# Moving SBUF buffers by 64 and 128 bytes in a three-block fp32 network: what the phase of an operand is worth

## The chip, the cores and the metric

The kernel runs on one core of a Trainium2 chip. The metric is the device time of one execution in microseconds (us). The three runs of the kernel before took 1833.24, 1834.17 and 1839.31 us, median 1834.17 us.

## What is computed

Three network blocks follow one another on the same 256 tokens of width 1024, in float32. Cut to its core, the reference is:

```python
x = first_block(x, c, ctx, ...)   # modulation, w_in and w_out, retention, then the expert part:
    gate, idx = lax.top_k(jnp.swapaxes(aff, 1, 2), cap)          # 16 experts take 32 tokens each
    a = jnp.einsum('becd,edf->becf', xs, w_gate)                 # 1024 -> 2048
    u = jnp.einsum('becd,edf->becf', xs, w_up)
    y = jnp.einsum('becf,efd->becd', jax.nn.silu(a) * u, w_down)
x = second_block(x, ...)          # state-space and recurrent branches, then a 3072-wide FFN
return third_block(x, ...)        # gated linear + sliding-window attention, then block attention
```

Outside the experts the work is dense products `h @ W` with W of 1024 rows, for all 256 tokens. The experts need 16 x 24 MB of weights, once each.

## The kernel before, in words

**A weight unit.** A dense matrix is cut into units of 1024 rows by 128 columns: eight tiles of 128x128, 4 KB per partition. Four units are one block of 2 MB. Blocks come through `ring`, four slots of 16 KB per partition, by DMA from the SP queue, in one fixed order.

**Two halves of a number.** TensorE multiplies in its rounded form of float32 (fp32r). To keep the precision, weights and activations are each split in a rounded high part and the rest. ScalarE writes a unit's high part from `ring` into one of the four buffers of `w_high` (line 2121 is the helper that records all of ScalarE's operations), VectorE then overwrites the unit in `ring` with its low part (lines 2437 and 2448). The activation's high part lies in `HH` (h_high in the trace), its low part in `H` (h_normed); further on both lie in `U` (work), in some norms in `SQ` (squares).

**A narrow unit.** `dense_unit` then makes 24 matmuls of 256 columns: eight with `w_high` as stationary operand on the high activations, eight with `w_high` on the low ones, eight with the low weights in `ring` on the high ones. The activations (1 KB per partition and tile) are the moving operand. `dense_together` does the same for several units tile by tile. There are 5616 such matmuls; all matmuls of these helpers stand at line 1644.

**A wide unit.** `dense_tokens` turns the roles round: 128 tokens of the activation are stationary, and the weights of four units are the moving operand, four runs of 128 columns (512 in all). There are 192 of these, and 48 with two units (256 columns).

**The experts.** Lines 2077, 2057 and again 1644: plain float32, the activations of 32 tokens stationary in `work` and `ring` moving, 512 columns.

**Where the buffers lie.** `sb` and `sb_split` take SBUF from a rising address, one buffer behind the other in the order of the calls; a buffer of 64 bytes per partition that nothing reads (`between_tables`, `behind_weights`) only moves what lies behind it. Inside a buffer every tile step is a multiple of 512 bytes, so that all tiles of a buffer have the buffer's phase modulo 256. The order of instructions on every engine is written out by hand and waits on semaphores; no address takes part in it.

Of the kernel before, what the change touches and what calls it, by code (L numbers as in the profile page):

```python
# [12 lines left out]
U32 = mybir.dt.uint32  # L13
# [4 lines left out]
P = 128  # L18
SEQ = 256
DM = 1024  # L20
KT = DM // P
# [3 lines left out]
EXPERTS = 16  # L25
CAP = 2 * SEQ // EXPERTS
# [66 lines left out]
HIGHS = 4  # L93
# [58 lines left out]
def d1_block(unit):  # L152

    return FIRST.index(("dense", unit // UNITS))
# [7 lines left out]
def block_ends(unit):  # L162
    return unit % UNITS == UNITS - 1
# [26 lines left out]
def program(nc, d, out):  # L190
    ctx = ExitStack()
    with ctx:
        def sb(name, shape, dt=F32):
            return ctx.enter_context(nc.sbuf_tensor(name, shape, dt))

        rounded = {}

        def sb_split(name, shape):

            buffer = sb(name, shape)  # L200
            size = 4 * math.prod(shape[1:])
            rounded[name] = nc.alloc_sbuf_tensor_at(name + "_rounded", shape, F32R, offset=nc.sbuf_base - size)
            return buffer
# [3 lines left out]
        B = [ctx.enter_context(nc.psum_tensor(f"bank{i}", [P, 512], F32)) for i in range(8)]  # L207

        ring = sb_split("ring", [P, RING, BLK])
        params = sb("params", [P, P_COLS])  # L210
        consts = sb("consts", [P, C_COLS])
        sb("between_tables", [P, 16])
        X = sb("x_resid", [P, KT, SEQ])
        H = sb_split("h_normed", [P, KT, SEQ])
        SQ = sb_split("squares", [P, KT, SEQ])
        RS = sb("rstd", [P, 2, SEQ])
        U = sb_split("work", [P, 80 * SEQ])
        ones = sb("ones", [P, P])
        sm = sb("small", [P, 844])
        w_high_plain = sb_split("weights_high", [P, HIGHS, KT * P])  # L220
        w_high = rounded["weights_high"]
        sb("behind_weights", [P, 16])
        idx_u = sb("topk_index", [EXPERTS, CAP], U32)
        HH_plain = sb_split("h_high", [P, KT, SEQ])
        HH = rounded["h_high"]

        def par(name, a=None, b=None):
            at, n = P_AT[name]
            return params[:, at + (0 if a is None else a):at + (n if b is None else b)]
# [5 lines left out]
        def tiles(a, n):  # L235
            return U[:, a * SEQ:(a + n) * SEQ]
# [4 lines left out]
        def small(at, n):  # L241
            return sm[:, at:at + n]
# [17 lines left out]
        def by_tile(ap):  # L260
            return [ap[:, k, :] for k in range(ap.shape[1])]
# [5 lines left out]
        def as_r(ap):  # L267

            return bass.AP(rounded[ap.tensor.name], ap.offset, ap.ap)
# [54 lines left out]
        ROT = tiles(76, 4)  # L324
        KW = SQ[:, :, :].rearrange("p (s t x) n -> p s t (x n)", s=2, t=TT)
        SFB = tiles(76, 4).rearrange("p (s h c) -> p s h c", s=2, h=HEADS1)
# [40 lines left out]
        w_room = w_high_plain[:, :, :].rearrange("p n c -> p (n c)")  # L367
        h_high, squares, h_normed = (a[:, :, :].rearrange("p k t -> p (k t)") for a in (HH_plain, SQ, H))
        AHEAD = ((w_room[:, 0:DEXP], w_room[:, DEXP:2 * DEXP]), (tiles(64, 8), tiles(72, 8)),
# [14 lines left out]
        I_OF = (8, 9, 10, 11, 76, 77, 78, 79)  # L384
        XDT = SQ[:, :, :].rearrange("p (t x) n -> p t (x n)", t=TT)
        DTT = small(112, 32).rearrange("p (t h) -> p t h", t=TT)
# [31 lines left out]
        def d2_block(unit):  # L418
            return D2_BLOCK0 + unit // UNITS
# [33 lines left out]
        def tensor_block2(pe, mm, dense_unit, dense_together, added_token_sums, spread_roots):  # L453
            def unit2(unit, act, name=None):
                tensor_dense2(pe, dense_unit, unit, act, PU2 + unit, base=IN_AT[name][0] if name else None)

            normed = by_tile(HH), by_tile(as_r(H[:, :, :]))

# [68 lines left out]
            for g in range(2):  # L527
                last = mm(B[4 + g][:, 0:SEQ], ones[:], SQ[:, 4 * g, :])
            last.then_inc(s.ya_sum, 1)
            for n in range(5, 8):  # L530
                unit2(L_LRU + n, lru)
            ssm = by_tile(as_r(SQ[:, :, :])), by_tile(as_r(YA))
            for n in range(8):
# [25 lines left out]
        def scalar_block2(act, fn, link, square, squares_of_x, raw_splits, root_table, root, unit_done, weight_high, split_high):  # L559
# [95 lines left out]
            for n in range(4):  # L655
# [6 lines left out]
                if n == 2:  # L662
                    act.wait_ge(s.ya_gated, 1)
                    fn(flat(SQ), tiles(53, 8), ACT.Square).then_inc(s.ya_act, 1)
                if n < 3:
# [62 lines left out]
        def vector_block2(dve, v, link, norm_invert, norm_to, add_normed, split_low, split_scaled_low, weight_low, weights_low):  # L728
# [182 lines left out]
            dve.wait_ge(s.dense_sb, PU2 + L_UP)  # L911
            add_normed(6, MO2, after=lambda k: split_scaled_low(H[:, k, :], X[:, k, :], par("ffn_pre", k, k + 1), HH_plain[:, k, :]))
            weight_low(L_UP - 1 + AHEAD2)
# [43 lines left out]
            dve.wait_ge(s.dense_sb, PU2 + L_DOWN + KT)  # L957
            add_normed(8, DO, after=lambda k: split_scaled_low(H[:, k, :], X[:, k, :], EVEN_GAIN[:, k:k + 1], HH_plain[:, k, :]))
            weight_low(L_EVEN - 1 + AHEAD2)
# [44 lines left out]
        def tensor_block3(pe, mm, dense_unit, dense_together, dense_tokens, added_sums, added_token_sums, spread_roots):  # L1004
            normed = by_tile(HH), by_tile(as_r(H[:, :, :]))

# [163 lines left out]
        def scalar_block3(act, fn, link, squares_of_x, raw_splits, root_table, root, unit_done, weight_high, split_high, splits_apart):  # L1170
# [111 lines left out]
            for n in range(RAW_UNITS):  # L1282
                for k in (2 * n, 2 * n + 1):
                    split_high(HH[:, k, :], H[:, k, :])
                unit_done(d2_block(L_ODD + n), block_ends(L_ODD + n))
# [28 lines left out]
        def vector_block3(dve, v, link, norm_invert, norm_to, final_norm, split_low, split_scaled_low, times_rstd, weight_low, weights_low):  # L1314
# [161 lines left out]
            for k in range(KT):  # L1476
                if k + 1 < KT:
                    times_rstd(10, H, X, RAW_GAIN, k + 1).then_inc(s.act_full, 1)
                split_low(H[:, k, :], HH[:, k, :])
                if k % 2 == 0:  # L1480
# [161 lines left out]
        def _(pe):  # L1642
# [196 lines left out]
            def first_jobs():  # L1839

                ctx_base, x_base = IN_AT["ctx"][0], IN_AT["x"][0]
                ctx_high, ctx_low = by_tile(as_r(CTXR)), by_tile(as_r(HC))
                x_high, x_low = by_tile(HH), by_tile(as_r(H[:, :, :]))
                by_unit = lambda ap: ap.rearrange("p (u k c) -> p u k c", u=UNITS, k=KT)
# [37 lines left out]
            for pu, (unit, act, t) in enumerate(DENSE1):  # L1882
# [3 lines left out]
                blk, sub = d1_block(unit), unit % UNITS  # L1886
                high, low = (HH, H[:, :, :]) if act == "x" else (as_r(CTXR), HC)
                high, low = by_tile(high), by_tile(as_r(low))
# [990 lines left out]
```

## Time and profile before

| what | value |
|---|---|
| median of three runs | 1834.17 us |
| the profiled execution, its own time | 1832.58 us |
| its span in the trace | 1830.8 us |
| TensorE matmuls busy | 80% of the span |
| VectorE, ScalarE, GpSimd busy | 39%, 32%, 2% |
| first stretch, first block's dense work | 0 to about 230 us |
| experts | about 250 to 1130 us |
| second and third block | about 1130 us to the end |

TensorE's row counts a matmul as busy from its start to the end of its pipeline, so that neighbours overlap; the pace of a train of matmuls is read from the starts of two rows and the number of matmuls between them. In the list of rows by time a row merges neighbouring instructions of one kind: its start, its length, and how many.

### The profile page before, as it was taken

The page shows a single profiled execution, that of the slowest core. Times are in us where ns is not written, and L with a number is a line of the kernel's source. Part 1 is how long each engine was busy: PE and PEld are TensorE (multiplying, and loading weights), DVE is VectorE, ACT ScalarE, POOL GpSimd, SP SyncE. Part 2 cuts the span into 40 slices and gives each one's busy share as a digit, 9 for nine tenths or more (in the row PEclk, how much of TensorE's full clock was granted, in tenths as well). Part 3 has the DMA queues.
Part 4 walks back from the last instruction along what each step waited for, and adds up shares of the span by engine and source line. Part 5 has one row for each costly group of instructions (what it writes and reads, how often), then busy time and mean ns, then how long its engine had stood idle before and what let it go on. Part 6 is the DMA issues. An engine that isn't in the chain of part 4 may idle for free.

```text
span 1830.8 us, 25067 instructions
## 1 busy us (share of the span) xinstructions
PE 1462.0 (80%) x10432; PEld 990.6 (54%) x10432; DVE 710.5 (39%) x1256; ACT 589.2 (32%) x1007; POOL 35.6 (2%) x40
## 2 busy tenths in 40 slices
PE   6999996665656666666656667999999999999998
PEld 4787941211112111112111112998998999999997
DVE  4457610000000000000000000897995999478764
ACT  6444510000000000000000001677475776465654
POOL 0000200000000000000000000000000000000101
PEclk9999897888887787877878877999999999999999
DMA  9566799999999999999999999657453755554330
GB/s 399 221 246 235 301 386 424 428 428 429 429 429 428 428 429 428 429 428 428 428 429 429 429 428 427 242 188 207 154 185 132 267 206 190 191 173 173 139 139 24
DMA packets 53266, 573.55 MB, mean 313 GB/s; under 512 B 4928, under 2 KB 15424, under 8 KB 16576
## 3 DMA queue, kind: packets, MB, share of 16 engines
q1 hardware_dynamic: 47440, 563.10, 75.7%
q10 hardware_dynamic: 5744, 9.28, 1.4%
q8 instruction: 61, 1.00, 0.2%
q14 instruction: 21, 0.17, 0.0%
HBM read 568.04 MB, written 4.33 MB: 313 GB/s over the span
## 4 chain that ended last, share of the span: by engine, by line
DMA 43%; PE 37%; DVE 16%; ACT 2%; issue 1%; SPq 0%; DVEq 0%; ACTq 0%
PE bank L1644 36%; DMA ring<-in_w_up 14%; DMA ring<-in_w_down 14%; DMA ring<-in_w_gate 13%; DVE ring_rounded L2437 6%; DVE work L929 2%; DVE work L747 1%; DMA ring<-in_dense 1%; DVE work L919 1%; DVE work_rounded L2360 1%; DMA work<-decay_rows 1%; ACT work L2121 1%; DVE work L738 1%; ACT weights_high_rounded L2121 1%; DMA ring<-in_w_ada 1%
## 5 line engine op out<-in xcount | busy, mean ns | idle before, releaser
L1644 PE MATMUL bank<-ring,work 128*32 128x512 f32 x3008 | 483.9, 778 | 293.5 <-DMA ring<-in_w_up 126.3
L1644 PEld LDWEIGHTS bank<-ring,work 128*32 128x32 f32 x3008 | 94.1, 127 | 646.8 <-DMA ring<-in_w_up 206.6
L2121 ACT ACTIVATE work<-bank 128x512 f32<-128x512 f32 (+3 forms) x152 | 72.8, 492 | 998.6 <-PE bank L1644 667.9
L2437 DVE TENSOR_TENSOR ring_rounded<-ring,weights_high_rounded 128x1024 fp32r<-128x1024 f32 x208 | 252.6, 1219 | 80.9 <-ACT weights_high_rounded L2121 80.9
L2121 ACT ACTIVATE weights_high_rounded<-ring 128x1024 fp32r<-128x1024 f32 x244 | 254.0, 1051 | 42.7 <-PE bank L1644 41.4
L2691 DVE TENSOR_TENSOR work<-work,bank 128x512 f32<-128x512 f32 x16 | 16.5, 1030 | 582.7 <-PE bank L1644 582.7
L1644 PE MATMUL bank<-h_high_rounded,weights_high_rounded 128*128 128x256 f32 x1264 | 185.5, 286 | 1.7 <-ACT h_high_rounded L2121 1.5
L1644 PE MATMUL bank<-h_high_rounded,ring_rounded 128*128 128x256 f32 x1264 | 174.5, 277 | 2.4 <-DVE ring_rounded L2448 2.4
L1644 PE MATMUL bank<-h_normed_rounded,weights_high_rounded 128*128 128x256 f32 x1264 | 173.7, 278 | 0.0
L1644 PEld LDWEIGHTS bank<-h_high_rounded,weights_high_rounded 128*128 128x128 f32 x1264 | 161.3, 188 | 13.2 <-issue 6.9
L1644 PEld LDWEIGHTS bank<-h_high_rounded,ring_rounded 128*128 128x128 f32 x1264 | 158.3, 188 | 2.9 <-DVE ring_rounded L2448 2.8
L1644 PEld LDWEIGHTS bank<-h_normed_rounded,weights_high_rounded 128*128 128x128 f32 x1264 | 157.9, 188 | 0.2
L1644 PE MATMUL bank<-work_rounded,weights_high_rounded 128*128 128x256 f32 x1152 | 152.1, 283 | 5.3 <-ACT work_rounded L2121 5.3
L1644 PEld LDWEIGHTS bank<-work_rounded,weights_high_rounded 128*128 128x128 f32 x1152 | 141.9, 192 | 9.4 <-ACT work_rounded L2121 6.9
L2705 DVE COPY work<-bank 128x512 f32<-128x512 f32 x16 | 11.1, 692 | 284.0 <-PE bank L1644 284.0
L2077 PE MATMUL bank<-work 128*128 128x256 f32 x256 | 70.1, 434 | 13.5 <-DVE work L2705 13.5
L2077 PEld LDWEIGHTS bank<-work 128*128 128x128 f32 x256 | 55.0, 221 | 44.2 <-issue 35.1
L1644 PE MATMUL bank<-work_rounded,ring_rounded 128*128 128x256 f32 x544 | 74.5, 280 | 0.0
L1644 PEld LDWEIGHTS bank<-work_rounded,ring_rounded 128*128 128x128 f32 x544 | 68.3, 191 | 0.0
L1627 POOL TENSOR_TENSOR squares<-squares 128x256 f32<-128x256 f32 x30 | 30.1, 1005 | 1770.8 <-ACT squares L2121 1770.8
L2448 DVE TENSOR_TENSOR ring_rounded<-ring,weights_high_rounded 128x1024 fp32r<-128x1024 f32 x36 | 43.6, 1221 | 44.1 <-ACT weights_high_rounded L2121 43.8
L2121 ACT ACTIVATE work<-work,params 128x256 f32<-128x256 f32 x85 | 48.5, 581 | 27.3 <-DVE work L738 17.8
(269 smaller groups left out, 1206.4 us busy)
## 6 DMA issues: line engine op xcount, KB each, us to landing
ring<-in_w_gate SPq DMA_DIRECT2D x63, 2048.0 KB, 16.2
ring<-in_w_down SPq DMA_DIRECT2D x63, 2048.0 KB, 16.2
ring<-in_w_up SPq DMA_DIRECT2D x61, 2048.0 KB, 16.3
ring<-in_dense SPq DMA_DIRECT2D x60, 2048.0 KB, 8.4
ring<-in_w_ada SPq DMA_DIRECT2D x12, 2048.0 KB, 13.5
work<-in_w_up SPq DMA_DIRECT2D x3, 1024.0 KB, 14.6
bias_diagonals<-work SPq DMA_DIRECT2D x2, 1536.0 KB, 14.9
ring<-in_dense SPq DMA_DIRECT2D x2, 1024.0 KB, 18.7
```

The source lines that it names most:

```text
L738: v.tensor_tensor(dst, B[(PU2 + u) % 4][:, 0:SEQ], RS[:, 1, :], ALU.mult).then_inc(s.dense_sb, 1)
L747: v.scalar_tensor_tensor(out=o[:, shift:SEQ], in0=SCALED2[:, u % 4, 0:SEQ - shift], scalar=w[:, 3 - shift:4 - shift], in1=o[:, shift:SEQ], ...
L919: v.tensor_tensor(SCALED[:, u % 4, :], B[(PU2 + L_UP + u) % 4][:, 0:SEQ], RS[:, 1, :], ALU.mult).then_inc(s.dense_sb, 1)
L929: v.scalar_tensor_tensor(out=o[:, shift:SEQ], in0=SCALED[:, u % 4, 0:SEQ - shift], scalar=ffn_weight(u, 2 - shift), in1=o[:, shift:SEQ], o ...
L1627: nc.gpsimd.tensor_tensor(SQ[:, 0, :], SQ[:, 0, :], SQ[:, k, :], ALU.add).then_inc(s.squares_added, 1)
L1644: return nc.tensor.matmul(o, lhsT, rhs, start=start, stop=stop)
L2077: last = nc.tensor.matmul(B[4 + k // 2][:, (k % 2) * SEQ:(k % 2 + 1) * SEQ], YE[:, k * P:(k + 1) * P], SELT[:], start=False, stop=final an ...
L2121: return nc.scalar.activation(o, i, f, **kw)
L2360: v.tensor_tensor(as_r(full), full, as_r(high) if high.dtype == F32 else high, ALU.subtract).then_inc(s.act_low, 1)
L2437: v.tensor_tensor(as_r(w), w, w_high[:, buffer, :], ALU.subtract).then_inc(s.w_low, 1)
L2448: v.tensor_tensor(as_r(w), w, w_high[:, unit % HIGHS, :], ALU.subtract).then_inc(s.w_low, 1)
L2691: v.tensor_tensor(HID.rearrange("p (i q) -> p q i", i=4), rows_apart(SG), rows_apart(B[1][:]), ALU.mult).then_inc(s.hid_ready, 1)
```

## The change

Buffers are allocated in another order, and the two unused 64-byte buffers are gone. Nothing else is edited: the list of instructions of every engine is the same row for row.

```diff
         ring = sb_split("ring", [P, RING, BLK])
+        w_high_plain = sb_split("weights_high", [P, HIGHS, KT * P])
+        w_high = rounded["weights_high"]
         params = sb("params", [P, P_COLS])
         consts = sb("consts", [P, C_COLS])
-        sb("between_tables", [P, 16])
+        idx_u = sb("topk_index", [EXPERTS, CAP], U32)
         X = sb("x_resid", [P, KT, SEQ])
         H = sb_split("h_normed", [P, KT, SEQ])
+        HH_plain = sb_split("h_high", [P, KT, SEQ])
+        HH = rounded["h_high"]
         SQ = sb_split("squares", [P, KT, SEQ])
         RS = sb("rstd", [P, 2, SEQ])
         U = sb_split("work", [P, 80 * SEQ])
         ones = sb("ones", [P, P])
         sm = sb("small", [P, 844])
-        w_high_plain = sb_split("weights_high", [P, HIGHS, KT * P])
-        w_high = rounded["weights_high"]
-        sb("behind_weights", [P, 16])
-        idx_u = sb("topk_index", [EXPERTS, CAP], U32)
-        HH_plain = sb_split("h_high", [P, KT, SEQ])
-        HH = rounded["h_high"]
```

The start of each buffer in a partition, in bytes, worked out from the sizes:

| buffer | before | modulo 256 | now | modulo 256 |
|---|---|---|---|---|
| ring | 16512 | 128 | 16512 | 128 |
| weights_high | 204544 | 0 | 82048 | 128 |
| params | 82048 | 128 | 98432 | 128 |
| consts | 85856 | 96 | 102240 | 96 |
| x_resid | 92096 | 192 | 108544 | 0 |
| h_normed | 100288 | 192 | 116736 | 0 |
| h_high | 221120 | 192 | 124928 | 0 |
| squares | 108480 | 192 | 133120 | 0 |
| rstd | 116672 | 192 | 141312 | 0 |
| work | 118720 | 192 | 143360 | 0 |
| ones | 200640 | 192 | 225280 | 0 |
| small | 201152 | 192 | 225792 | 0 |

## Rows read from the trace of the kernel before

**Rows 1.** Busy time of each engine in stretches (count in brackets), clock, DMA share, GB/s
```profile
0.00:100.00 100.00, 83.35 (x530) 63.14 (x534) 46.02 (x74) 52.09 (x97) 0.20 (x4) 1.00 0.77 312
100.00:230.00 130.00, 124.41 (x907) 109.56 (x897) 85.73 (x164) 57.85 (x109) 11.12 (x12) 0.95 0.65 257
250.00:1130.00 880.00, 557.28 (x3252) 157.77 (x3248) 32.69 (x61) 32.89 (x53) 0.00 (x0) 0.80 1.01 428
1130.00:1831.00 701.00, 677.67 (x5608) 654.11 (x5600) 543.03 (x951) 445.19 (x747) 24.26 (x24) 0.99 0.50 179
1450.00:1500.00 50.00, 50.00 (x444) 50.00 (x443) 48.95 (x95) 36.21 (x56) 0.00 (x0) 1.00 0.57 204
```

**Rows 2.** Costliest groups: busy us, mean ns | idle before, releaser
```profile
L1644 PE MATMUL bank<-ring,work 128*32 128x512 f32 x3008 | 483.9, 778 | 293.5 <-DMA ring<-in_w_up 126.3
...
L2437 DVE TENSOR_TENSOR ring_rounded<-ring,weights_high_rounded 128x1024 fp32r<-128x1024 f32 x208 | 252.6, 1219 | 80.9 <-ACT weights_high_rounded L2121 80.9
```

**Rows 3.** TensorE by time, a train of narrow units in work
```profile
1560.57 1.98 PE L1644 MATMUL bank<-work_rounded,weights_high_rounded 128*128 128x256 f32 x16
1562.39 1.07 PE L1644 MATMUL bank<-work_rounded,ring_rounded 128*128 128x256 f32 x8
1563.29 1.98 PE L1644 MATMUL bank<-work_rounded,weights_high_rounded 128*128 128x256 f32 x16
```

**Rows 4.** TensorE by time, another train, at 1628 us
```profile
1628.39 1.10 PE L1644 MATMUL bank<-h_normed_rounded,weights_high_rounded 128*128 128x256 f32 x8
1629.34 1.10 PE L1644 MATMUL bank<-h_high_rounded,ring_rounded 128*128 128x256 f32 x8
1630.28 1.10 PE L1644 MATMUL bank<-h_high_rounded,weights_high_rounded 128*128 128x256 f32 x8
1631.22 1.10 PE L1644 MATMUL bank<-h_normed_rounded,weights_high_rounded 128*128 128x256 f32 x8
```

**Rows 5.** Durations by buffer, ns min/median/max: 1628 to 1646 us, then 1426 to 1500 us
```profile
L1644 PE MATMUL bank<-h_normed_rounded,weights_high_rounded x54: 279/281/281, 1628.4 to 1645.9; 128*128 128x256 f32 x54
...
L1644 PE MATMUL bank<-h_normed_rounded,weights_high_rounded x216: 276/276/276, 1426.6 to 1498.1; 128*128 128x256 f32 x108
```

**Rows 6.** First and last longer train of the second kind, by time
```profile
102.28 1.10 PE L1644 MATMUL bank<-h_normed_rounded,weights_high_rounded 128*128 128x256 f32 x8
...
1768.15 1.11 PE L1644 MATMUL bank<-h_normed_rounded,weights_high_rounded 128*128 128x256 f32 x8
```

**Rows 7.** TensorE by time, wide units at 75 us
```profile
75.27 2.00 PE L1644 MATMUL bank<-weights_high_rounded,h_high_rounded 128*128 128x512 f32 x8
77.10 1.99 PE L1644 MATMUL bank<-weights_high_rounded,h_normed_rounded 128*128 128x512 f32 x8
78.93 2.03 PE L1644 MATMUL bank<-ring_rounded,h_high_rounded 128*128 128x512 f32 x8
80.80 2.00 PE L1644 MATMUL bank<-weights_high_rounded,h_high_rounded 128*128 128x512 f32 x8
```

**Rows 8.** Matmuls with two columns, by time, then their durations (ns min/median/max)
```profile
1685.42 1.84 PE L1644 MATMUL bank<-ones,work 128*128 128x2 f32 x16
...
L1644 PE MATMUL bank<-ones,work x16: 165/251/251, 1685.4 to 1687.0; 128*128 128x2 f32 x16
```

**Rows 9.** VectorE by line and shape: busy us, mean ns | idle before
```profile
L2360 DVE TENSOR_TENSOR work_rounded<-work,work_rounded 128x256 fp32r<-128x256 f32 x72 | 29.0, 418 | 3.4 <-ACT work_rounded L2121 3.2
```

**Rows 10.** The chain that ended last, 1130 us to the end, its share by line
```profile
by line: PE bank L1644 48.1%; DVE ring_rounded L2437 14.7%; DVE work L929 5.4%; DVE work L747 3.5%; DMA ring<-in_w_down 2.5%; issue 2.4%; DVE work L919 2.3%; DVE work_rounded L2360 1.9%; DMA work<-decay_rows 1.9%; DVE work L738 1.7%; DVE wo
```

**Rows 11.** DMA issues: count, KB each, median us from issue to landing
```profile
weights_high<-in_w_gate SPq DMA_DIRECT2D x2, 1024.0 KB, 10.2
...
h_high<-in_w_up SPq DMA_DIRECT2D x1, 1024.0 KB, 18.5
```

## The prediction, made before the changed kernel ran

> **What bounds the kernel now.** I read three views in this order. First the stretches [rows 1]: from 250 to 1130 us the DMA engines are full (share 1.01, 428 GB/s) while TensorE's weight loads are busy for only 158 of 880 us; from 1130 us to the end TensorE is busy for 678 of 701 us and the DMA half idle. So the experts are bound by the transfers, and what lies ahead of 230 us and behind 1130 us mostly by TensorE's instruction stream. Then the groups [rows 2]: in the experts the matmuls wait 293 us for the ring, so nothing that happens to their pace can show. Last the chain that ended last [rows 10]: of the 701 us behind the experts 48% are matmuls of line 1644, 15% VectorE's making of low weights, and the rest short steps of a norm or a scan. VectorE is a close second: between 1450 and 1500 us it is busy for 48.95 of 50 us [rows 1]. A faster TensorE would soon run into it there; a slower one would be paid nearly in full.
>
> **The change part by part.** No instruction, wait or transfer is added, removed or moved. What changes are starts modulo 256 bytes: the weights' high parts go from 0 to 128, the ring stays at 128, all activations go from 192 to 0. Five kinds of access could notice.
>
> *Narrow units, 5616 matmuls.* Their pace is read from starts. In [rows 3] 24 matmuls go from 1560.57 to 1563.29 us: 2.72/24 = 113.3 ns. In [rows 4] 24 go from 1628.39 to 1631.22: 2.83/24 = 117.9 ns. Both are uninterrupted trains at full clock, on the same buffers' phases. The duration marks the kinds as well: 276 ns in every matmul of the one, median 281 in the other [rows 5]. So there are two paces, and a train keeps the one with which it began until its next gap. Going through all starts in this manner I count 4089 gaps at the fast pace and 1285 at the slow one, which occurs from 101 to 1781 us [rows 6]; the rest are real waits. Within one train the pace does not change when the stationary operand goes from `w_high` at 0 to the ring at 128: in [rows 4] eight from the ring take 0.94 us (1629.34 to 1630.28) and eight from `w_high` take 0.94 us. Thus for narrow units half the change, 0 to 128 for `w_high`, is seen to be worth nothing against activations at 192. The other half, activations at 0, no narrow matmul of this trace shows.
>
> The bounds of it come from the nearest rows. Below: matmuls with two columns are paced by their weight loads alone, and 16 of them take (1.84 - 0.165)/15 = 111.7 ns each [rows 8]. If no moving read ever disturbed anything the narrow units would run at that: 4089 x 1.6 ns = 6.5 us and 1285 x 6.2 = 8.0 us, together 14.5 us. Above: if every train fell in the slow pace, 4089 x 4.6 = 18.8 us. The mean of wide units (below) per 256 columns, 117 ns at most, is no worse than that, so I take 118 as the upper bound of the pace.
>
> *Wide units, 192 matmuls.* Here a phase does show. With the activations stationary at 192 in all three rows, eight matmuls with `w_high` (0) moving take 1.83 us (75.27 to 77.10, and again to 78.93), 228.8 ns each, and eight with the ring (128) moving take 1.87 us (78.93 to 80.80), 233.8 ns [rows 7]. The change puts both at 128 against 0. I expect between 229 for all (64 x 5 ns = 0.3 us less) and 234 for all (128 x 5 = 0.6 us more): nothing, but it is the proof that the start of an operand modulo 256 can matter to TensorE at all, by some 2%.
>
> At this place a rule can be set against the rows. The Trainium skill, page "SBUF — State Buffer", section "SBUF: two separate sides", says that contention on the engines' side comes only from the port pair of VectorE and GpSimd and that TensorE never waits on anyone; "TensorE: Matmul & The Clock Gate", section "Step-by-step: what each phase is for", says that loading the next weights takes no read bandwidth from the running matmul. By these rules placement is worth exactly zero, which is the result of the first rival below too. The trace agrees only in part: with the same code the pace of wide units differs by 5 ns with the buffer read.
>
> *VectorE and ScalarE.* The low-weights step reads the ring (128) and `w_high` (0) and takes 1219 ns for 1024 elements [rows 2]; the same operation on activations (192 and 192) takes 418 ns for 256 [rows 9]. The difference is 801 ns for 768 elements, 1.04 ns each, in one straight line through two different pairs of phases, so I charge 0. After the change the two operands of the first are both at 128; were that to cost what it may, the equal phases of the second (192 and 192) bound it at nothing again.
>
> *Transfers.* The ring stays at its very address, so the experts' 880 us at 428 GB/s stay. Six of the 1 MB loads of the first expert change the phase of their target [rows 11]; they are queued in the saturated stretch's beginning, and a per cent of about 2.4 us each (1 MB at 428 GB/s) is 0.15 us: 0.
>
> *Experts' matmuls.* Their moving operand, the ring, stays, and their stationary one moves from 192 to 0; covered by 293 us of waiting for the ring [rows 2]. Cost 0.
>
> The sum for unchanged paces is thus 0 to -0.3 us on the profiled execution's 1832.58 us (span 1830.8 and 1.8 around it), and the median of the runs lies 1.6 us above that execution. Since which trains fall in the slow pace depends on how they start, I also expect a few us between executions. I say 1833 us.
>
> **The rivals.** What can be told from no change is about 0.3%, 5.5 us.
>
> *A, paces as now (the forecast), 0.38.* For it: 113.3 and 117.9 do not care about 0 or 128 on the stationary side, and both paces exist at one placement, so the start in time decides. Time 1829 to 1838.
>
> *B, activations at 0 are better, 0.32.* The slow pace vanishes, or the fast one drops toward 111.7. The first alone gives 1285 x 4.6 = 5.9 us; the long slow trains lie in stretches that the chain runs through TensorE, so most of it counts: 1828. Both together give at most 14.5 us, of which VectorE's limit around 1450 to 1550 takes a third: 1823 or so. For it: in wide units a moving operand at 0 is faster than one at 128. Against it: there the weights, now at 128, are what moves, and the fast pace stands only 1.6 ns above the load's own floor, so there is little to win.
>
> *C, they are worse, 0.30.* Weights at 128 and activations at 0 make the slow pace the one in which trains end. It decides from the point where over 30% of the 4089 fast gaps turn slow (30% x 18.8 = 5.6 us). Since TensorE is busy for 678 of 701 us, most counts: with all of them 18.8 x 0.8 = 15 us, 1849. For it: trains start slow and most of them only slip into the fast pace within three matmuls, so that the fast pace is a lock that a phase may prevent; before, activations and weights differed by 64 modulo 128, now by 0. Against it: the same trains ignore a shift of 128.
>
> **How the numbers follow.** A, B and C hold 0.38, 0.32 and 0.30. The range for 8 in 10 goes from B's 1824 to C's 1850. A's own range is 1829 to 1838. Faster by over 0.3%: most of B and a little of A, 0.32; slower by over 0.3%: most of C and a little of A, 0.29; the same 0.39.
>
> **What would show it.** Each step is read at its own place. The span of the experts (250 to 1130 us) must keep its length and its 428 GB/s. VectorE's 1219 ns and ScalarE's durations must stay. For the narrow units, look at the two paces and at how many matmuls have 281 in place of 276 ns: A says 276 and 281 with some 1300 of the second; B says no 281, or a duration below 276; C says thousands of 281, or a third value. For the wide units, both buffers must show one pace, as they now have one phase. The prediction would be wrong if a pace above 118 ns or below 113 appeared, or if the DMA's rate moved with the targets of the few early loads.

## The result, and the profile after

The changed kernel takes 1850.81 us (median of six runs, 1845.85 to 1855.23); the kernel before takes 1833.05 us in its six. The ratio is 1.009, 95% interval 1.0073 to 1.0106: slower by 0.9%, some 18 us. The profiled execution took 1855.23 us, the longest of its six, with a span of 1853.4 us: 22.6 us more than the one of before. What is read from the two traces below adds up to these 22.6 us, not to the 18.

Busy time by stretch, in the changed kernel (as in [rows 1]: the stretch, its length, then PE, PEld, DVE, ACT, POOL with their counts, the clock, the DMA share and GB/s):

```profile
300.00:1100.00 800.00, 496.35 (x2903) 134.09 (x2904) 30.24 (x56) 24.48 (x41) 0.00 (x0) 0.80 1.01 429
1140.00:1854.00 714.00, 696.32 (x5600) 674.10 (x5596) 545.68 (x951) 446.51 (x747) 24.39 (x24) 0.99 0.49 175
1450.00:1500.00 50.00, 50.00 (x424) 50.00 (x423) 48.70 (x92) 35.91 (x55) 0.00 (x0) 1.00 0.50 177
```

The experts move the same 429 GB/s. In the stretch from 1450 to 1500 us TensorE is never idle, at full clock, in either kernel, but it starts 424 matmuls where it started 444: its stream is slower. By the starts of the matmuls, the first expert matmul comes at 235.1 us (before 230.3), the last at 1149.0 (1139.8), TensorE's last matmul of all 698.2 us behind that (684.8): 4.9 us are lost ahead of the experts, 4.3 in them, 13.5 behind them.

TensorE by time, the changed kernel (start, length, and what):

```profile
1500.32 1.11 PE L1642 MATMUL bank<-h_high_rounded,weights_high_rounded 128*128 128x256 f32 x8
1501.26 1.12 PE L1642 MATMUL bank<-h_normed_rounded,weights_high_rounded 128*128 128x256 f32 x8
1502.22 1.11 PE L1642 MATMUL bank<-h_high_rounded,ring_rounded 128*128 128x256 f32 x8
1503.17 1.11 PE L1642 MATMUL bank<-h_high_rounded,weights_high_rounded 128*128 128x256 f32 x8
```

From 1500.32 to 1503.17 are 24 matmuls in 2.85 us: 118.8 ns each. In [rows 3] it was 113.3, in [rows 4] 117.9. It is a third pace, and the durations (ns min/median/max, here of one group between 1450 and 1600 us) show it as well:

```profile
L1642 PE MATMUL bank<-h_high_rounded,ring_rounded x304: 279/281/285, 1451.0 to 1557.2; 128*128 128x256 f32 x152
```

The 276 ns that marked the fast pace [rows 5] are gone; within a train the distances between starts now go through 115 to 122 ns in a pattern that repeats. The mean over all uninterrupted narrow matmuls (those whose successor starts within 130 ns) is 118.75 ns; before it was 114.5. The wide units have one pace now, eight in 1.86 us (232.5 ns), where [rows 7] had 228.8 and 233.8:

```profile
75.61 2.02 PE L1642 MATMUL bank<-weights_high_rounded,h_high_rounded 128*128 128x512 f32 x8
77.47 2.02 PE L1642 MATMUL bank<-weights_high_rounded,h_normed_rounded 128*128 128x512 f32 x8
79.33 2.02 PE L1642 MATMUL bank<-ring_rounded,h_high_rounded 128*128 128x512 f32 x8
```

The two other engines' rows stand: the low-weights step of VectorE is charged 1220 ns (1219 before), ScalarE's high-weights step 1051 ns (1051).

```profile
L2435 DVE TENSOR_TENSOR ring_rounded<-ring,weights_high_rounded 128x1024 fp32r<-128x1024 f32 x208 | 252.8, 1220 | 87.6 <-ACT weights_high_rounded L2119 87.5
L2119 ACT ACTIVATE weights_high_rounded<-ring 128x1024 fp32r<-128x1024 f32 x244 | 254.2, 1051 | 49.1 <-PE bank L1642 48.6
```

And the chain that ended last, behind the experts, its share by line:

```profile
by line: PE bank L1642 88.2%; DMA ring<-in_w_down 2.4%; DVE ring_rounded L2435 1.3%; ACT weights_high_rounded L2119 0.9%; ACT work L2119 0.9%; issue 0.9%; PE bank L1038 0.6%; DVE work_rounded L2358 0.6%; ACT squares L2119 0.5%; DVE rstd L88
```

In [rows 10] TensorE held 48.1% of it and VectorE's low weights 14.7%; now 88.2% and 1.3%. VectorE used to be a second limit in places; a slower TensorE has left it behind.

### The profile page after: what moved, and what is told of

Its sections match the earlier page's. It is cut to its first block, busy times and chain, and to the rows that moved or that the text cites. A ratio compares the mean times of both kernels' runs of the same rounds, so it can differ in the third digit from the quotient of the medians.

```text
span 1853.4 us, 25067 instructions
## 1 busy us (share of the span) xinstructions
PE 1483.0 (80%) x10432; PEld 1011.4 (55%) x10432; DVE 713.5 (38%) x1256; ACT 590.6 (32%) x1007; POOL 35.6 (2%) x40
## 4 chain that ended last, share of the span: by engine, by line
PE 52%; DMA 42%; DVE 3%; ACT 2%; issue 1%; SPq 0%; ACTq 0%; DVEq 0%
PE bank L1642 51%; DMA ring<-in_w_down 14%; DMA ring<-in_w_up 13%; DMA ring<-in_w_gate 13%; DMA ring<-in_dense 1%; DMA ring<-in_w_ada 1%; DVE ring_rounded L2435 1%; DVE ring_rounded L2446 0%; ACT work L2119 0%; ACT weights_high_rounded L2119 0%; DVE work_rounded L2358 0%; PE bank L2075 0%; PE bank L1038 0%; ACT squares L2119 0%; ACT L2119 0%
## 5 line engine op out<-in xcount | busy, mean ns | idle before, releaser
L2435 DVE TENSOR_TENSOR ring_rounded<-ring,weights_high_rounded 128x1024 fp32r<-128x1024 f32 x208 | 252.8, 1220 | 87.6 <-ACT weights_high_rounded L2119 87.5
L2119 ACT ACTIVATE weights_high_rounded<-ring 128x1024 fp32r<-128x1024 f32 x244 | 254.2, 1051 | 49.1 <-PE bank L1642 48.6
L1642 PE MATMUL bank<-h_high_rounded,weights_high_rounded 128*128 128x256 f32 x1264 | 190.9, 290 | 1.7 <-ACT h_high_rounded L2119 1.7
L1642 PE MATMUL bank<-h_high_rounded,ring_rounded 128*128 128x256 f32 x1264 | 181.0, 283 | 2.1 <-DVE ring_rounded L2446 2.1
L1642 PE MATMUL bank<-h_normed_rounded,weights_high_rounded 128*128 128x256 f32 x1264 | 179.8, 283 | 0.0
L1642 PEld LDWEIGHTS bank<-h_high_rounded,weights_high_rounded 128*128 128x128 f32 x1264 | 165.7, 189 | 13.1 <-issue 6.6
L1642 PEld LDWEIGHTS bank<-h_high_rounded,ring_rounded 128*128 128x128 f32 x1264 | 164.2, 190 | 2.6 <-DVE ring_rounded L2446 2.5
L1642 PEld LDWEIGHTS bank<-h_normed_rounded,weights_high_rounded 128*128 128x128 f32 x1264 | 163.1, 189 | 0.2
L2075 PE MATMUL bank<-work 128*128 128x256 f32 x256 | 66.8, 420 | 13.5 <-DVE work L2703 13.5
## 6 DMA issues: line engine op xcount, KB each, us to landing
ring<-in_w_down SPq DMA_DIRECT2D x63, 2048.0 KB, 16.4
```

The costliest lines, as they stand in the source:

```text
L1642: return nc.tensor.matmul(o, lhsT, rhs, start=start, stop=stop)
L2075: last = nc.tensor.matmul(B[4 + k // 2][:, (k % 2) * SEQ:(k % 2 + 1) * SEQ], YE[:, k * P:(k + 1) * P], SELT[:], start=False, stop=final an ...
L2119: return nc.scalar.activation(o, i, f, **kw)
L2435: v.tensor_tensor(as_r(w), w, w_high[:, buffer, :], ALU.subtract).then_inc(s.w_low, 1)
```

## The experiments

Theories at the start: D, the distance (start of the moving minus start of the stationary operand) modulo 128 decides; M, the activations' own phase decides; W, the high weights' move did it. All kernels differ from the changed one only in the order and the unused bytes of the allocation, and were run beside the kernel before on the same chip. Ratios are to that kernel.

**e1: only the high weights' move is left** (ring 128, high weights 128, activations 192).

```diff
-        idx_u = sb("topk_index", [EXPERTS, CAP], U32)
+        sb("pad3", [P, 16])
         X = sb("x_resid", [P, KT, SEQ])
...
         sm = sb("small", [P, 844])
+        idx_u = sb("topk_index", [EXPERTS, CAP], U32)
```

> The changed kernel with the activations (and all that lies behind them) back at 192 modulo 256, by 64 unused bytes; ring and high weights stay at 128. Of the change only the high weights' move from 0 to 128 is left. Theory D (what counts is the distance of moving and stationary operand modulo 128: 64 is good, 0 is bad) and theory M (what counts is the activations' own phase, 192 good and 0 bad) both expect the time of before, 1833 us, with narrow units in two paces, 113.3 and 117.8 ns. Theory W (the high weights' move did it) expects the changed kernel's 1851 us and its mixed pace of about 119 ns.

Measured: 1844.84 us against 1834.55, ratio 1.0056 (1.0036 to 1.0077). No theory had said that: it is neither the old time nor the new one. The activations are back at 192 and 10 us of the loss remain, so M falls as the whole cause, and D with it. Its durations between 1500 and 1600 us:

```profile
L1643 PE MATMUL bank<-work_rounded,weights_high_rounded x295: 279/279/280, 1548.3 to 1599.9; 128*128 128x256 f32 x148
...
L1643 PE MATMUL bank<-h_high_rounded,ring_rounded x140: 279/279/280, 1499.8 to 1548.2; 128*128 128x256 f32 x140
```

It is the slow pace almost everywhere (mean 117.5 ns; the fast one in 7% of the matmuls, 76% before). The 7% are not strays: a train of 94 matmuls at 89 us runs at the fast pace from end to end. The 279 ns were seen in the kernel before too, there only in the thirds of slow trains that read the ring, while the thirds with high weights had 281. The ring's distance, 192 - 128 = 64, is what both buffers have in e1.

**e2: only the activations' move is left** (ring 128, high weights 0, activations 0).

```diff
         ring = sb_split("ring", [P, RING, BLK])
+        sb("pad1", [P, 32])
...
-        idx_u = sb("topk_index", [EXPERTS, CAP], U32)
...
         sm = sb("small", [P, 844])
+        idx_u = sb("topk_index", [EXPERTS, CAP], U32)
```

> The high weights back at 0 modulo 256, the ring at 128, activations at 0 as in the changed kernel. Theories D and M expect 1851 us and about 119 ns per narrow matmul for both stationary buffers. Theory W expects 1833 us, or 113.3 ns at least for the 16 of 24 matmuls that read the high weights.

Measured: 1851.76 us, ratio 1.0106 (1.0077 to 1.0134). W falls as the whole cause: the activations' move alone costs 17 us. The matmuls with high weights (distance 0) take 119.6 ns, those with the ring (distance 128, as in the changed kernel) 118.1 ns.

**e3: activations at 64** (ring and high weights 128).

```diff
         idx_u = sb("topk_index", [EXPERTS, CAP], U32)
+        sb("pad3", [P, 16])
```

> Ring and high weights at 128, activations at 64. The distance is 64 modulo 128 again, but the activations' own phase is one that no run has had. Theory D expects 1833 us and the paces 113.3 and 117.8 ns. Theory M says nothing of 64 for certain; a time away from 1833 us speaks for it and against D. If the distance counts modulo 256, 192 here is what the high weights had before, and the ring's 64 is gone.

Measured: 1832.76 us against 1834.55, ratio 0.9998 (0.9983 to 1.0014): the time of before. TensorE by time:

```profile
1500.74 1.07 PE L1643 MATMUL bank<-h_high_rounded,ring_rounded 128*128 128x256 f32 x8
1501.65 1.07 PE L1643 MATMUL bank<-h_high_rounded,weights_high_rounded 128*128 128x256 f32 x8
1502.55 1.07 PE L1643 MATMUL bank<-h_normed_rounded,weights_high_rounded 128*128 128x256 f32 x8
1503.46 1.07 PE L1643 MATMUL bank<-h_high_rounded,ring_rounded 128*128 128x256 f32 x8
```

24 matmuls in 2.72 us, 113.3 ns: the fast pace is back, in 64% of all. The distance is 64 - 128, that is 192 modulo 256. e1 and e3 have the same distance modulo 128 and differ by 12 us, which settles it against D in its form modulo 128; 64 and 192 are not the same.

**e4: all at 128**, distance 0.

```diff
-        idx_u = sb("topk_index", [EXPERTS, CAP], U32)
...
         sm = sb("small", [P, 844])
+        idx_u = sb("topk_index", [EXPERTS, CAP], U32)
```

> All at 128: distance 0. Theory D expects the changed kernel's time, 1851 us, and about 119 ns. If the distance counts modulo 256, equal phases may be worse than the 128 of the changed kernel: above 1855 us. Theory M: anything, if the activations' phase 128 differs from 0.

Measured: 1855.84 us, ratio 1.0124 (1.0096 to 1.0153), the slowest. TensorE by time, one train, then wide units:

```profile
1500.12 1.12 PE L1642 MATMUL bank<-h_normed_rounded,weights_high_rounded 128*128 128x256 f32 x8
1501.08 1.12 PE L1642 MATMUL bank<-h_high_rounded,ring_rounded 128*128 128x256 f32 x8
1502.04 1.12 PE L1642 MATMUL bank<-h_high_rounded,weights_high_rounded 128*128 128x256 f32 x8
1503.00 1.12 PE L1642 MATMUL bank<-h_normed_rounded,weights_high_rounded 128*128 128x256 f32 x8
...
77.65 1.98 PE L1642 MATMUL bank<-weights_high_rounded,h_normed_rounded 128*128 128x512 f32 x8
79.46 1.98 PE L1642 MATMUL bank<-ring_rounded,h_high_rounded 128*128 128x512 f32 x8
```

24 narrow ones in 2.88 us, 120.0 ns, the worst pace; yet the wide ones, 1.81 us for eight, 226 ns by these rows and 227.7 over all, are the best of any kernel. After these four the theory became D256: the pace depends on the distance of the moving to the stationary start modulo 256, apart for narrow and for wide units.

**e5: everything 128 further on** (ring and high weights 0, activations 192; distance 192 as in e3).

```diff
+        sb("pad0", [P, 32])
         ring = sb_split("ring", [P, RING, BLK])
...
+        sm = sb("small", [P, 844])
         params = sb("params", [P, P_COLS])
...
-        sm = sb("small", [P, 844])
```

> Ring and high weights both at 0, activations at 192: the distance of moving to stationary operand in narrow units is 192 modulo 256, as in the run with weights at 128 and activations at 64, but every buffer lies 128 further on modulo 256. Theory D256 (only the distance modulo 256 counts) expects that run's narrow paces, 113.3 and 117.8 ns with matmul durations of 276 and 281 ns and a mean near 115, and wide units at 229 ns. Theory A (each buffer's own phase counts) expects other paces. Beside this the ring now starts at a multiple of 256: if the transfers cared for it, the 428 GB/s of the experts would rise; a share of 1.5% would be 13 us less, 1820 us. If they don't, 1833 us.

Measured: 1829.20 us against 1833.22, ratio 0.9981 (0.9968 to 0.9993). Narrow units have a mean of 115.1 ns (e3: 115.0), wide ones 229.2 (229.1): D256 holds. By the sizes of the buffers the narrow distance modulo 512 is 448 in e3 and 192 here, so a longer period than 256 is not needed. And the time is a little under that of before, which brings up the transfers (e9 to e12).

**e6 and e7: steps of 32 bytes** (activations at 96 and at 32).

```diff
         idx_u = sb("topk_index", [EXPERTS, CAP], U32)
+        sb("pad3", [P, 24])      # e6; 8 in e7
```

> A finer step: weights at 128, activations at 96, distance 224, half way between 192 (fast and slow pace, mean 115.0 ns) and 0 (119.9 ns). If the distance acts in steps of 64 bytes the run is like one of its neighbours to 0.2 ns: 1833 or 1856 us. If it acts evenly, the mean is 117 to 118 ns and the time about 1844 us.

> Weights at 128, activations at 32, distance 160, between 128 (118.7 ns, 1851 us) and 192 (115.0 ns, 1833 us). In steps of 64 bytes it is like one of these; evenly, 117 ns and 1842 us. Wide units have distance 96, between 229.1 and 232.4 ns.

Measured: 1846.35 us, ratio 1.0080 (1.0063 to 1.0097), mean pace 118.3 ns; and 1846.40 us, 1.0081 (1.0052 to 1.0109), 117.8 ns. Neither is like a neighbour, and neither has the fast pace. In time they lie near what an even course gives (e7's four runs go from 1841 to 1855 us), but both paces lie above it, which gives 117 to 118 for e6 and 117 for e7. e7's wide units, 233.3 ns, lie outside the 229.1 to 232.4 that were expected.

**e8: a good and a bad third** (high weights 192, activations 128, ring 128).

```diff
         ring = sb_split("ring", [P, RING, BLK])
+        sb("pad1", [P, 16])
...
+        sm = sb("small", [P, 844])
         params = sb("params", [P, P_COLS])
...
-        sm = sb("small", [P, 844])
```

> Mixed: high weights at 192 and activations at 128 (distance 192, the good one), ring at 128 (distance 0, the worst). If each matmul's pace is set by its own distance, the 16 of 24 with high weights run at 113.3 or 117.8 ns and the 8 with the ring at 119.9: mean about 116.8, some 1842 us. If a train's pace is a lock that one bad third breaks, the high weights' matmuls never reach 113.3 and the mean is 118.5 to 120, 1850 us and more.

Measured: 1846.86 us, ratio 1.0078 (1.0062 to 1.0094). Durations between 1500 and 1600 us:

```profile
L1643 PE MATMUL bank<-h_normed_rounded,weights_high_rounded x144: 281/281/282, 1500.3 to 1549.4; 128*128 128x256 f32 x144
...
L1643 PE MATMUL bank<-h_high_rounded,ring_rounded x144: 281/283/284, 1501.3 to 1550.4; 128*128 128x256 f32 x144
```

Half of each answer: in the same train the high weights' matmuls run at their own distance's slow pace (mean 117.5 ns, duration 281) and the ring's at theirs (119.4, duration 283), so each has its own; but the fast pace is down to 6%, so the bad third does break the lock. The kernel before shows the other side of it: there the ring's third had distance 64, and in trains whose other two thirds had 192 it ran at the fast pace too ([rows 3], mean 114.5 ns), where e1, all at 64, has 117.5. A matmul's own distance is thus not the whole of it; that of its neighbours in the train counts as well.

**e9 to e12: the ring's place, twice two.** e9 has ring, high weights and activations all at 0; e10 is e4 again, e11 is e5, e12 is e3.

```diff
+        sb("pad0", [P, 32])                                   # e9
         ring = sb_split("ring", [P, RING, BLK])
...
-        idx_u = sb("topk_index", [EXPERTS, CAP], U32)
...
         sm = sb("small", [P, 844])
+        idx_u = sb("topk_index", [EXPERTS, CAP], U32)
```

> The worst distance, 0, with all at 0 in place of all at 128: ring, high weights and activations at 0 modulo 256. Theory R (a ring at a multiple of 256 is filled faster) expects the experts some 5 us shorter and the time some 5 us under the run with all at 128, so about 1851 us against 1856. Theory D256 alone expects the same narrow pace of 119.9 ns and the same time, 1856.

> Once more ring, high weights and activations all at 128, on the same chip as the run with all at 0: 1856 us, 119.9 ns per narrow matmul, 428 to 429 GB/s in the experts.

> Once more ring and high weights at 0, activations at 192 (distance 192), to see the gain of 3.5 us over the kernel before again: theory R expects 430 GB/s or more in the experts and 1829 us; if the gain was chance, 1833 us.

> Once more ring and high weights at 128, activations at 64: the same distance 192 with the ring at its old place. Theory R expects 429 GB/s in the experts and about 5 us more than its partner with the ring at 0; otherwise the two are equal.

| kernel | ring | distance | us | ratio to before (95%) | experts, us | behind them, us |
|---|---|---|---|---|---|---|
| e9 | 0 | 0 | 1848.45 | 1.0084 (1.0071 to 1.0098) | 904.3 | 701.2 |
| e10 | 128 | 0 | 1857.11 | 1.0135 (1.0118 to 1.0152) | 910.5 | 701.4 |
| e11 | 0 | 192 | 1829.33 | 0.9979 (0.9969 to 0.9990) | 905.4 | 686.2 |
| e12 | 128 | 192 | 1833.52 | 1.0009 (0.9995 to 1.0022) | 910.6 | 682.5 |

The stretch from 300 to 1100 us, in this order e9, e10 and e2:

```profile
300.00:1100.00 800.00, 491.35 (x2916) 133.81 (x2920) 30.23 (x56) 24.48 (x41) 0.00 (x0) 0.81 1.01 431
```

```profile
300.00:1100.00 800.00, 492.04 (x2900) 132.22 (x2904) 30.25 (x56) 24.48 (x41) 0.00 (x0) 0.81 1.01 429
```

```profile
300.00:1100.00 800.00, 493.90 (x2904) 135.45 (x2896) 30.26 (x56) 24.48 (x41) 0.00 (x0) 0.81 1.01 429
```

With the ring at a multiple of 256 the transfers run at 431 in place of 429 GB/s and the experts are 5 to 6 us shorter, at either distance; e9 and e10 agree behind the experts to 0.2 us. All eleven profiles with the ring at 128, before and after included, have 909.5 to 913.8 us there, the three with the ring at 0 have 904.3 to 905.4. The layout of e5 and e11 beats the kernel before, twice, by 0.2%. That it is the ring, and not another of the buffers moved with it, is shown by e2 and e9: they differ in nothing but whether the 128 unused bytes lie ahead of the ring or behind it, so that every other buffer has the same address in both. e2 (ring at 128) has 429 GB/s and 912.2 us of experts, e9 (ring at 0) 431 GB/s and 904.3. In the whole time e9 lies 8.7 us under e10, more than the 5 that theory R expected and the 6.2 of its experts; the rest is not explained.

The Trainium skill, page "DMA: Bandwidth & Descriptors", section "How a descriptor splits into AXI transactions", says that a descriptor that starts off a 256-byte boundary costs extra beats. It words this for what is read; here it is the written side that moved. All the data packets of these transfers are of 16 KB in the trace. If each is one descriptor, its rule gives 516 beats for 512 when it starts 128 bytes off: an estimate of 0.8%, 7 us of 910. The traces agree in sign and about in size: 5.2 us between e12 and e11, 6.2 between e10 and e9, 7.9 between e2 and e9.

## Why the prediction was wrong

All profiles but e8's together, by the distance of the moving to the stationary start modulo 256 (means over uninterrupted matmuls, ns):

| distance | narrow units | wide units |
|---|---|---|
| 0 | 119.9 (e4, e9, e10), 119.6 (e2, high weights) | 227.7 (e4), 227.9 (e2, high weights) |
| 32 | | 233.2 (e6) |
| 64 | 117.5 (e1), 114.5 (before, ring: one third of trains with two thirds at 192) | 229.1 (e3), 229.2 (before, high weights) |
| 96 | | 233.3 (e7) |
| 128 | 118.75 (after), 118.1 (e2, ring) | 232.3 (after), 232.5 (e2, ring) |
| 160 | 117.8 (e7) | |
| 192 | 114.8 to 115.1 (e3, e5, e11, e12), 114.4 (before, high weights) | 233.3 (e1), 233.7 (before, ring) |
| 224 | 118.3 (e6) | |

The mixed kernel e8 fits the table in its narrow units (117.5 at 192 and slow, 119.4 at 0), less well in its wide ones: 230.3 at 64 and 229.7 at 0, where the pure layouts have 229.1 and 227.7.

Another engine's accesses, whose phases moved as well, do not make the loss. In e4's trace 84 narrow matmuls have VectorE, ScalarE and GpSimd idle from 100 ns ahead of them to 100 ns behind and no transfer's packet under way: their mean is 119.9 ns, that of all. In the changed kernel 83 such have 119.0 (all: 118.75), in the kernel before 57 have 113.9 (all: 114.5).

**The forecast was A, and rival C came nearest.** The change puts every narrow matmul at distance 128, where before two thirds had 192 and a third 64. The fast pace is gone from the trains, as C said, and C's 1849 us is close. But they do not end in the slow pace: they run at a third one, 118.75 ns, which C allowed as a sign and did not price. And C's reason, 64 modulo 128 before and 0 now, fell with e1. So the nearness of C's time is in part luck.

**The activations' half was priced at nothing without a row: this step failed.** The prediction says itself that no narrow matmul of its trace shows activations at 0, and its sum then takes the paces as unchanged, 0 to -0.3 us. e2, which has this half alone, takes 17.2 us more than the kernel before, nearly all of the 18.

**"Half the change, 0 to 128 for the high weights, is worth nothing": this step failed too.** Its observation was right: within one train the pace does not change with the stationary buffer. But it looked only at trains already in one of the two paces. What the phase decides is whether a train gets into the fast one, and by e1 that fell from 76 to 7% of the matmuls when the high weights went from 0 to 128: 10 us by that half alone. The two halves, 10 and 17 us, do not add up to the 18 of both; with the activations at 0 the high weights' place makes no difference in time that can be told (e2 1851.76 us, the changed kernel 1850.81, not run side by side). A property that keeps itself cannot be priced from how it behaves once it is there.

**"I take 118 as the upper bound of the pace": too low.** The changed kernel has 118.75 and e4 119.9. The bound was taken from the two paces of one layout and from half a wide matmul; the table shows that narrow and wide do not follow one another: distance 0 is the worst for the one and the best for the other. Hence the upper end of the range, 1850 us, lay 0.8 us under the median.

**"A slower one would be paid nearly in full": 64%.** Behind the experts the uninterrupted narrow matmuls take 562.0 us in place of 540.9, 21.1 more. The stretch is only 13.5 longer. The sum of the distances over 260 ns from a narrow matmul's start to the next, the real waits, fell from 24.9 to 16.4 us: a slower TensorE comes later to the places where it had to wait. Whose steps these waits were for was not told apart. The shares of the chain fit this: TensorE's went from 48.1 to 88.2%, that of VectorE's low weights from 14.7 to 1.3%. Ahead of the experts 768 narrow matmuls by 4.0 ns (118.8 against 114.8 there) give 3.1 of the 4.9 us; the rest is within what two executions of one layout differ by there (first expert matmul at 233.0 us in e3, at 229.6 in e12).

**Wide units: right.** Priced at -0.3 to +0.6 us and taken as the proof that the phase matters; 232.3 lies between the 229 and 234 given. (The sum then carries only the -0.3 of it, and says 1833 us where it gives about 1834; neither matters beside the 18 us.)

**VectorE, ScalarE, transfers, experts' matmuls: right at nothing**, by their rows above. That VectorE's two rows lie "in one straight line" was no evidence, since any two points do; the 1220 against 1219 ns after the change is. The early 1 MB loads that change their target's phase are eight by the trace of before and not six, which moves no figure. The 4.3 us within the experts are not explained: 913.8 is 2.5 us above the middle of the kernels with the ring at 128, and the 909.5 of before is their lowest.

**Placement worth nothing**, which the prediction drew from two rules (the Trainium skill, "SBUF — State Buffer", section "SBUF: two separate sides", and "TensorE: Matmul & The Clock Gate", section "Step-by-step: what each phase is for"), does not hold for these rounded matmuls: with one and the same code, TensorE's pace goes from 115.0 to 119.9 ns with the distance of its two operands. That it is the weight load of the next matmul that meets the moving read of the running one fits the rows, the shift of e5 above all, but no run has the one without the other: this is argued, not shown, and so it is open which of the two rules fails, if either does. Open also is what makes a train at distance 192 slow in one execution or place and fast in another (the same 95 matmuls at about 50 us are at the fast pace to 95% in e3 and not at all in e12, which is the same kernel), and why 64 hardly ever gets there.

## What to carry to other kernels

When TensorE's stream is the limit and the operands are in the rounded form, the starts of the stationary and the moving buffer modulo 256 bytes are a tuning knob: here up to 4% of the pace of narrow units (115.0 to 119.9 ns) and 1.5% of the time (1829 to 1857 us). Read the pace from the starts of long trains, and try the distances 0, 64, 128 and 192, for each width of matmul by itself. Give both stationary buffers of a train the same good distance: e8, with one third at a bad one, took 14 us more than the kernel before. Before pricing a layout from the trace of another, ask whether a pace seen there is a state that keeps itself: then its share, not its size, is the unknown. And try the buffer that the big transfers fill at a multiple of 256 bytes: here this was worth 5 to 8 us of 910.

## What the runs showed that was not expected

The same train of matmuls has two steady paces at full clock, 113.3 and 117.8 ns, at one and the same layout, and keeps the one that it has after its first few matmuls, in the kernel before for 1153 matmuls in a row at the longest. Distances of 32 bytes off the multiples of 64 cost wide units 4 to 5 ns (233.2 and 233.3 against 227.7 and 229.1), so that the course between is not even.
